# Unread products in TensorE's waits, and another order of the routing and of the last expert

## Chip, cores and metric

One core of one Trainium2 chip runs the program. The metric is the time of one execution on the device, in microseconds. Every time below is of the kernel before.

## What is computed

The reference is a stack of layers over 512 tokens of 1024 channels: a pooling layer and a latent-attention layer, each followed by a SwiGLU, a final norm, then differential attention and a routed mixture of experts. The change lies in the last part, which starts where differential attention has its heads:

```python
o = rmsnorm(o, subln) * (1 - lambda_init)          # 8 heads of 128
x = x + o.reshape(B, T, 1024) @ w_out              # da_out
xt = rmsnorm(x, norm_ffn)
logit_g, logit_e = xt @ w_group + b_group, xt @ w_router + b_router   # 4 groups, 16 experts
# the best group, the two best of its four experts, with shares
for e in range(16):
    y += combine[:, e] * ((silu(xt @ w_gate[e]) * (xt @ w_up[e])) @ w_down[e])   # 1024 -> 512 -> 1024
out = x + y
```

Everything is f32. Each weight product is made of three TensorE products: an operand is split into a high part (f32r) and the rest, and `product` adds low x high, high x low and high x high (lines 255 to 257), each 128 rows of weights against 512 columns.

## The kernel before

The 512 tokens are four tiles (T = 4) of 128. Every engine has its own list of instructions, written out by hand, and they meet by semaphores. PS is PSUM, eight banks of 512 columns. X holds the tokens.

**Attention's end and da_out.** VectorE scales the heads of a tile in two parts (`normal_part`, line 1776: six heads and two), in the order (0,0), (1,0), (2,0), (0,1), (1,1), (3,0), (2,1), (3,1) for (tile, part). TensorE turns each part into PS as it comes (line 1828). ScalarE copies a whole turned tile to AH (line 1837, high parts), VectorE makes AL (line 1846, low parts), and `route` starts the products of the output projection when tile 0 is there. They go tile by tile over four units of weights (`unit_into`, `unit_half`).

**Routing.** As tiles get ready, VectorE adds the residual (lines 2139, 2148), TensorE turns X (`turn_x`, line 1998) and makes 20 logits per token (`logits`, line 2007). The last tile is done in two halves. VectorE selects (`select`) and finds each token's place in its experts' lists (`place`) for a pair of tiles at a time. TensorE counts the places (lines 2047 to 2071) and turns them into a table of token numbers (`table`, line 2016) and a table of shares (line 2077). `row(t)` (line 2159) makes the normalized rows of tile t, which SyncE stores to moe_rows (line 1968) for the experts to gather; x_out (line 1964) stores X. `counts` holds the number of turns through the experts, one for these inputs; each engine loads it into a register (line 2327) and loops over it.

**Experts.** Six units of 1 MB of weights per expert (two each for gate, up and down), 96 in all. Eight are fetched in advance, and SyncE fetches another when VectorE has split the one in its slot (line 2339). ScalarE makes the high parts, `hi(k)` (line 2424), VectorE the low ones, `lo(k)` (line 2486), TensorE multiplies (`half_up` and `down`, 12 products a unit). GpSimd gathers 128 rows per expert (lines 2555, 2559), TensorE turns them (`turn_rows`, line 2357), ScalarE and VectorE copy high and low parts (`rows_out`, lines 2428 and 2491). ScalarE applies Silu (2435), VectorE multiplies gate by up (`gate_up`, 2498), TensorE turns h (`turn_h`, 2380), both copy it (`h_out`, 2439 and 2502), and after down ScalarE scales by the shares (`y_out`, 2445) and GpSimd adds the rows to the output (2570). Unit numbers: gate 88 and 89, down of expert 14 90 and 91, up 92 and 93, down 94 and 95 for the last expert.

The first steps of the experts' loop before are these, ScalarE above and VectorE below:

```python
hi(0); hi(1); hi(2); rows_out(0); hi(3); silu(0); rows_out(1); hi(4)
lo(0); lo(1); rows_out(0); lo(2); lo(3); rows_out(1)
```

VectorE comes to its lo(0) only after it has waited for the table of shares, copied it and loaded its count (lines 2293 to 2295, 2327).

Of the kernel before, what the change touches and what calls it, by code (L numbers as in the profile page):

```python
# [36 lines left out]
P = 128  # L37
# [8 lines left out]
SLOTS = 2  # L46
# [131 lines left out]
def build_program(nc, stream, experts, x, positions, gains, rows, lams, router, consts, band, out, moe_rows):  # L178
    ctx = ExitStack()
    with ctx:  # L180
# [78 lines left out]

        def square_tile(act, b, n, t, junk=None):  # L260
# [1555 lines left out]
        def da_out(block, O, normal):  # L1816
# [7 lines left out]
            def _(pe):  # L1824
                for n, (t, part) in enumerate(((0, 0), (1, 0), (2, 0), (0, 1), (1, 1), (3, 0), (2, 1), (3, 1))):
# [4 lines left out]
                    if part:  # L1830
                        mm.then_inc(heads_turned, 1)

# [26 lines left out]
        def expert_memory():  # L1859
# [43 lines left out]
            m.slot_share = sb("slot_share", [P, ROUNDS + 1, E])  # L1903
# [8 lines left out]

            m.prefetch = prefetch
            return m


        def route(block, m, qk_used, weighed, made, heads_lo):
# [27 lines left out]
            weight_ready = sem("expert_weight_ready")  # L1945
            u0 = U_DA_OUT
            last = T - 1
            ALF = AL[:, :, :].bitcast(F32)

# [32 lines left out]
            def _(pe):  # L1982
# [73 lines left out]
                turn_x(last, 0)  # L2056
                turn_x(last, 1)
# [4 lines left out]

# [8 lines left out]
                mm.then_inc(ranked, 1)  # L2071
                table(1).then_inc(tabled, 1)

# [8 lines left out]
            def _(act):  # L2082
# [36 lines left out]
                act.activation(m.group_exp[:, :, :], m.group_less[:, :, :], ACT.Exp).then_inc(exped, 1)  # L2119
                act.wait_ge(exp_ready, 2)  # L2120
# [3 lines left out]
            def _(dve):  # L2124
# [109 lines left out]
                invert(2)  # L2234
                row(2)
# [10 lines left out]
                dve.tensor_tensor(rstd[:, last:T], m.halves[:, 0:1], m.halves[:, 1:2], ALU.add).then_inc(sum_added, 1)  # L2246
                logit(2)
# [28 lines left out]
                dve.memset(m.slot_share[:, ROUNDS, :], 0.0)  # L2276
# [16 lines left out]
                dve.wait_ge(shares_tabled, 1)  # L2293
                then(dve.tensor_copy(m.slot_share[:, 0:ROUNDS, :].rearrange("p r e -> p (r e)"), PS[:, 7, 0:ROUNDS * E]))
                dve.tensor_copy(m.share_now[:, :], m.slot_share[:, 0, :]).then_inc(weight_ready, 1)

            return counted, index_ready, weight_ready, rows_stored, x_stored


        def run_experts(block, m, counted, index_ready, weight_ready, rows_stored, x_stored):  # L2300
# [22 lines left out]
            found, y = X[:, 0:2, :], X[:, 2:4, :]  # L2323

            def rounds_of(engine):
                engine.wait_ge(counted, 1)
                return engine.value_load(counts[0:1, 0:1], min_val=1, max_val=ROUNDS)
# [16 lines left out]
            def _(pe):  # L2344
                rounds = rounds_of(pe)
                with nc.Fori(0, rounds, engines=(mybir.EngineType.PE,), hint_back_edge=True) as r:
# [49 lines left out]
                    turn_rows(0)  # L2396
                    gate(0, 0)
                    gate(0, 1)
                    turn_rows(1)
                    for n in range(E):  # L2400
                        for part in range(2):
                            half_up(n, PS[:, 1, :], up_unit(n), part)
                        if n + 1 < E:
                            gate(n + 1, 0)
                        turn_h(n)
                        if n + 1 < E:
                            gate(n + 1, 1)
# [250 lines left out]
```

## Time and profile before

| | us |
|---|---|
| median of 3 runs | 1569.75 |
| lowest and highest | 1566.68, 1569.96 |
| the profiled execution's own time | 1566.38 |
| its span, first to last instruction | 1564.6 |
| attention, da_out and all before it | to 1181.5 |
| output projection and routing | 1181.5 to 1249.9 |
| experts' first product to last | 1260.7 to 1553.6 |
| last rows added, end | 1553.6 to 1564.6 |

Mean granted TensorE clock: 0.981 of full speed. The profile's times are from the span's start. The clock has two levels, 1.0 for 2.4 GHz and 0.5 for 1.2 GHz; a value between means that it changed in the stretch. A busy TensorE at the low level does half as much.

### The profile page before, as it was taken

To read this page: it belongs to the slowest core of one execution; us is meant where nothing else is said; L and a number is where in the kernel's file an instruction comes from. 1 tells how busy PE (TensorE), PEld (TensorE's weight loads), DVE (VectorE), ACT (ScalarE), POOL (GpSimd) and SP (SyncE) were. 2 spreads that over 40 slices of the span, in tenths; PEclk is the share of its full clock that TensorE was granted. 3 is DMA by queue.
4 is the path that set the end of the run, shared out by engine and by line. 5 is a ranking of instruction groups with operands and counts; after the bars stand their busy time and mean duration, and the time that the engine had idled before them with its cause. 6 is when DMAs were issued, how large, how long until landed. Compare 5 with 4: busy or idle time off the path is not lost.

```text
span 1564.6 us, 19025 instructions
## 1 busy us (share of the span) xinstructions
PE 1504.3 (96%) x7399; PEld 1244.3 (80%) x7399; DVE 780.5 (50%) x947; ACT 673.8 (43%) x854; POOL 79.5 (5%) x57
## 2 busy tenths in 40 slices
PE   8899999999899999999999999999899789999996
PEld 8888888888787788888888887788567778888874
DVE  6433333231566435333323216335684679899884
ACT  5322222212355424222322115433782368787773
POOL 0000000000000000000000000000130012111211
PEclk9999999999999999999999999999999789999998
DMA  6123232232230032323232232232132379999993
GB/s 243 61 101 107 80 107 85 104 104 98 81 108 28 1 121 67 115 88 107 80 107 105 84 121 81 98 108 81 33 120 120 149 273 384 384 390 393 387 380 96
DMA packets 36207, 226.18 MB, mean 145 GB/s; under 512 B 5271, under 2 KB 5527, under 8 KB 11824
## 3 DMA queue, kind: packets, MB, share of 16 engines
q1 hardware_dynamic: 31392, 212.06, 35.9%
q0 software_dynamic: 4608, 13.22, 3.6%
q8 instruction: 45, 0.74, 0.2%
q14 instruction: 18, 0.15, 0.0%
q10 hardware_dynamic: 144, 0.03, 0.0%
HBM read 215.22 MB, written 13.63 MB: 146 GB/s over the span
## 4 chain that ended last, share of the span: by engine, by line
PE 53%; DVE 5%; DMA 3%; issue 2%; ACT 2%; DVEq 0%; ACTq 0%; SPq 0%; POOLq 0%
PE PS L255 16%; PE PS L257 16%; PE PS L256 16%; DMA eraw<-experts 3%; PE PS L1648 1%; PE PS L2357 1%; DVE da_flat L1732 1%; PE PS L1659 1%; DVE WL L250 1%; PE PS L2007 1%; ACT WEH L2424 1%; PE PS L1668 1%; PE PS L1453 0%; DVE da_flat L1746 0%; DVE WEL L2486 0%
## 5 line engine op out<-in xcount | busy, mean ns | idle before, releaser
L250 DVE TENSOR_TENSOR WL<-raw,WH 128x2048 fp32r<-128x2048 f32 x93 | 213.9, 2300 | 432.1 <-ACT WH L245 432.1
L255 PE MATMUL PS<-AH,WL 128*128 128x512 f32 (+1 forms) x768 | 286.7, 373 | 4.3 <-DVE AL L303 4.3
L256 PE MATMUL PS<-AL,WH 128*128 128x512 f32 (+1 forms) x768 | 286.0, 372 | 0.0
L257 PE MATMUL PS<-AH,WH 128*128 128x512 f32 (+1 forms) x768 | 286.0, 372 | 0.0
L245 ACT ACTIVATE WH<-raw 128x2048 fp32r<-128x2048 f32 x93 | 177.6, 1910 | 240.9 <-PE PS L257 240.9
L2486 DVE TENSOR_TENSOR WEL<-eraw,WEH 128x2048 fp32r<-128x2048 f32 x96 | 217.2, 2286 | 20.1 <-ACT WEH L2424 19.9
L2424 ACT ACTIVATE WEH<-eraw 128x2048 fp32r<-128x2048 f32 x96 | 182.2, 1914 | 31.6 <-DMA eraw<-experts 16.7
L255 PEld LDWEIGHTS PS<-AH,WL 128*128 128x128 f32 x768 | 145.6, 190 | 29.5 <-DVE AL L303 4.5
L257 PEld LDWEIGHTS PS<-AH,WH 128*128 128x128 f32 x768 | 145.5, 189 | 25.2
L256 PEld LDWEIGHTS PS<-AL,WH 128*128 128x128 f32 x768 | 145.6, 190 | 24.9
L255 PE MATMUL PS<-WH,AL 128*128 128x512 f32 (+2 forms) x416 | 156.3, 376 | 8.0 <-DVE WL L250 7.6
L257 PE MATMUL PS<-WH,AH 128*128 128x512 f32 (+2 forms) x416 | 154.1, 371 | 0.0
L256 PE MATMUL PS<-WL,AH 128*128 128x512 f32 (+2 forms) x416 | 153.8, 370 | 0.0
L255 PE MATMUL PS<-WEH,AH 128*128 128x512 f32 x256 | 102.7, 401 | 5.5 <-DVE AH L2491 5.5
L257 PE MATMUL PS<-WEH,AH 128*128 128x512 f32 x256 | 100.9, 394 | 0.0
L256 PE MATMUL PS<-WEL,AH 128*128 128x512 f32 x256 | 100.6, 393 | 0.0
L255 PEld LDWEIGHTS PS<-WH,AL 128*128 128x128 f32 x416 | 79.3, 191 | 22.2 <-DVE WL L250 6.8
L257 PEld LDWEIGHTS PS<-WH,AH 128*128 128x128 f32 x416 | 79.3, 191 | 13.0
L256 PEld LDWEIGHTS PS<-WL,AH 128*128 128x128 f32 x416 | 79.4, 191 | 12.1
L255 PE MATMUL PS<-WH,f0FL 128*128 128x512 f32 x176 | 69.8, 396 | 0.0
L257 PE MATMUL PS<-WH,f0FH 128*128 128x512 f32 x176 | 69.6, 395 | 0.0
L256 PE MATMUL PS<-WL,f0FH 128*128 128x512 f32 x176 | 69.6, 395 | 0.0
(316 smaller groups left out, 2110.2 us busy)
## 6 DMA issues: line engine op xcount, KB each, us to landing
eraw<-experts SPq DMA_DIRECT2D x96, 1024.0 KB, 14.6
raw<-stream SPq DMA_DIRECT2D x94, 1024.0 KB, 4.8
out<-X SPq DMA_DIRECT2D x5, 512.0 KB, 2.7
moe_rows<-moe_rows_g SPq DMA_DIRECT2D x5, 512.0 KB, 2.7
X<-x SPq DMA_DIRECT2D x4, 512.0 KB, 5.3
ffn_row<-rows SPq DMA_DIRECT2D x2, 512.0 KB, 9.3
final_row<-rows SPq DMA_DIRECT2D x2, 512.0 KB, 6.0
cst<-consts SPq DMA_DIRECT2D x1, 739.5 KB, 13.5
```

What stands on the lines that cost most here:

```text
L245: act.activation(WH[:, u % SLOTS, :], raw[:, u % SLOTS, :], ACT.Copy).then_inc(unit_hi, 1)
L250: dve.tensor_tensor(WL[:, u % SLOTS, :], raw[:, u % SLOTS, :], WH[:, u % SLOTS, :].bitcast(F32), ALU.subtract).then_inc(unit_lo, 1)
L255: pe.matmul(acc, lhs_lo, rhs_hi, start=start, stop=False)
L256: pe.matmul(acc, lhs_hi, rhs_lo, start=False, stop=False)
L257: return pe.matmul(acc, lhs_hi, rhs_hi, start=False, stop=stop)
L1648: pe.matmul(PS[:, 2 * (i % 2) + m, 0:(q + 1) * P], QT[rows64, h, q * P:(q + 1) * P], KT[rows64, h, 0:(q + 1) * P], start=True, stop=True). ...
L1659: mm = pe.transpose(PS[:, 4 + j % 2, k * P:(k + 1) * P], buffer(j, 0)[:, k * P:(k + 1) * P], ident)
L1668: mm = pe.matmul(PS[:, 6 + h % 2, q * P:(q + 1) * P], turned_probs[:, j % 2, k * P:(k + 1) * P], V[:, k, h * P:(h + 1) * P], start=(k == 0 ...
L1732: dve.tensor_tensor_reduce(buffer(i, m), PS[:, 2 * (i % 2) + m, 0:w], const("alibi")[:, S - w:S], 2.0 ** (-8.0 * (h + 1) / H), -NEG * 1e8, ...
L2007: mm = pe.matmul(PS[:, 2 * t, 0:20], m.XT[:, t, c, :], m.wr[:, c, :], start=(c == 0), stop=(c == C - 1))
L2424: act.activation(WEH[:, k % ESLOTS, :], eraw[:, k % ERAW, :], ACT.Copy).then_inc(unit_hi, 1)
L2486: dve.tensor_tensor(WEL[:, k % ESLOTS, :], eraw[:, k % ERAW, :], WEH[:, k % ESLOTS, :].bitcast(F32), ALU.subtract).then_inc(unit_lo, 1)
```

## The change

It adds `keep_busy`: n products of 128 by 512 whose result nothing reads, written to a bank of PS that is not in use. Eight places call it, with 7, 2, 2, 5, 9, 6, 4 and 6 products, 41 in all. The other edits: `invert(2)` and `row(2)` move on VectorE from ahead of `place(0)` to behind the sums of the last tile; the table of shares is no longer copied to SBUF whole, but read from PS at the start of each turn through the experts; ScalarE loads its count earlier; `rows_out(0)` goes ahead of `hi(2)` and of `lo(1)`; in the last expert `hi(95)` goes ahead of `y_out(14)`, and `lo(95)` behind `gate_up` and `h_out`. The diff, cut to its core:

```diff
+        def keep_busy(pe, bank, n, some=None):
+            some = AL[:, 3, :] if some is None else some
+            for _ in range(n):
+                pe.matmul(PS[:, bank, :], some[:, 0:P], some[:, 0:512], start=True, stop=True)
...
@@ da_out, TensorE, after the turn of each (tile, part)
+                    if n == 2:
+                        pe.wait_ge(unit_lo, u0 + 1)
+                        keep_busy(pe, 6, 7, WH[:, u0 % SLOTS, :])
...
@@ expert_memory
-            m.slot_share = sb("slot_share", [P, ROUNDS + 1, E])
...
@@ route, TensorE
                 turn_x(last, 0)
+                keep_busy(pe, 0, 2, WH[:, (u0 + 3) % SLOTS, :])
                 turn_x(last, 1)
                 for t in (2, last):
                     logits(t, 0)
                     logits(t, 1)
                 table(0)
-
+                keep_busy(pe, 0, 2)
                 pe.wait_ge(selected, 3)
...
                 mm.then_inc(ranked, 1)
+                keep_busy(pe, 0, 5)
                 table(1).then_inc(tabled, 1)
-
+                keep_busy(pe, 0, 9)
                 pe.wait_ge(weighted_out, 1)
...
@@ route, ScalarE
                 act.activation(m.group_exp[:, :, :], m.group_less[:, :, :], ACT.Exp).then_inc(exped, 1)
+                act_rounds.append(m.rounds_of(act, counted))
                 act.wait_ge(exp_ready, 2)
...
@@ route, VectorE
                 select(0)
-                invert(2)
-                row(2)
                 place(0)
                 add_half(0)
...
                 dve.tensor_tensor(rstd[:, last:T], m.halves[:, 0:1], m.halves[:, 1:2], ALU.add).then_inc(sum_added, 1)
+                invert(2)
+                row(2)
                 logit(2)
...
-                dve.memset(m.slot_share[:, ROUNDS, :], 0.0)
...
                 ins.then_inc(weighted_out, 1)
-                dve.wait_ge(shares_tabled, 1)
-                then(dve.tensor_copy(m.slot_share[:, 0:ROUNDS, :].rearrange("p r e -> p (r e)"), PS[:, 7, 0:ROUNDS * E]))
-                dve.tensor_copy(m.share_now[:, :], m.slot_share[:, 0, :]).then_inc(weight_ready, 1)
...
@@ run_experts, TensorE
                     turn_rows(0)
+                    keep_busy(pe, 0, 6)
                     gate(0, 0)
...
+                        if n == E - 1:
+                            keep_busy(pe, 3, 4)
                         turn_h(n)
+                        if n == E - 1:
+                            keep_busy(pe, 3, 6)
...
@@ run_experts, ScalarE
-                rounds = rounds_of(act)
-                with nc.scalar.Fori(0, rounds) as r:
+                with nc.scalar.Fori(0, act_rounds) as r:
...
                     hi(1)
+                    rows_out(0)
                     hi(2)
-                    rows_out(0)
                     hi(3)
...
                     for n in range(E):
+                        after = up_unit(n) + 2
+                        if n == E - 1:
+                            hi(after + 1)
                         if n:
                             y_out(n - 1)
...
                         else:
-                            hi(after + 1)
                             h_out(n)
...
@@ run_experts, VectorE
                     lo(0)
+                    rows_out(0)
                     lo(1)
-                    rows_out(0)
+                    dve.wait_ge(shares_tabled, 1)
+                    dve.wait_ge(y_made, E * r + 1)
+                    dve.tensor_copy(share[:, :], shares[:, bass.ds(r, 1), :].rearrange("p r e -> p (r e)")
+                                    ).then_inc(weight_ready, 1)
                     lo(2)
...
                             lo(after)
-                            lo(after + 1)
                             gate_up(n)
                             h_out(n)
+                            lo(after + 1)
...
-                    dve.wait_ge(y_made, E * r + E + 1)
-                    dve.tensor_copy(share[:, :], m.slot_share[:, bass.ds(r + 1, 1), :].rearrange("p r e -> p (r e)")
-                                    ).then_inc(weight_ready, 1)
```

## Rows read from the trace of the kernel before

**Rows 1.** The page's part 1: busy us, share of the span and instructions of each engine.

```profile
PE 1504.3 (96%) x7399; PEld 1244.3 (80%) x7399; DVE 780.5 (50%) x947; ACT 673.8 (43%) x854; POOL 79.5 (5%) x57
```

**Rows 2.** The chain that ended last, in order: start us, us, what, xcount if merged.

```profile
1223.53 1.71 PE PS L2007 x16
...
1265.35 0.43 PE PS L256
...
1266.48 0.23 PE PS L256
```

**Rows 3.** Busy time by stretch: us, each engine's busy (x), PEclk, DMA share, GB/s.

```profile
1174.10:1177.40 3.30, 1.50 (x12) 1.03 (x11) 3.02 (x14) 0.42 (x2) 0.00 (x0) 1.00 0.93 360
1177.50:1180.80 3.30, 3.30 (x17) 3.10 (x16) 2.96 (x6) 1.84 (x2) 0.00 (x0) 0.50 1.02 415
...
1235.50:1241.10 5.60, 4.61 (x22) 4.48 (x22) 1.88 (x9) 2.63 (x3) 0.00 (x0) 0.50 0.47 187
...
1260.70:1266.10 5.40, 5.38 (x13) 4.22 (x14) 4.28 (x2) 0.00 (x0) 0.00 (x0) 0.50 0.98 357
...
1276.00:1530.00 254.00, 253.08 (x1198) 209.24 (x1197) 226.36 (x130) 202.27 (x144) 50.79 (x26) 1.00 1.02 385
...
1546.10:1549.40 3.30, 2.88 (x7) 2.33 (x8) 0.32 (x1) 0.00 (x0) 0.00 (x0) 0.50 0.00 0
```

**Rows 4.** Timeline of da_out: start us, us, engine line op out<-in xcount [idle before].

```profile
1177.17 4.10 PE L1828 MATMUL PS<-cst,da_flat 128*128 128x128 f32 x20 [1.54 <-DVE da_flat L1776]
...
1177.47 2.30 DVE L1776 TENSOR_TENSOR da_flat<-da_flat,da_head_stat 128x256 f32<-128x256 f32 x5
1178.96 4.25 ACT L1837 ACTIVATE AH<-PS,gain 128x1024 fp32r<-128x1024 f32 x4 [2.38 <-PE PS L1828]
...
1180.11 4.86 DVE L1846 SCALAR_TENSOR_TENSOR AL<-PS,gain,AH 128x1024 fp32r<-128x1024 f32 x4 [0.34 <-ACT AH L1837]
```

**Rows 5.** Timeline of the routing's end, columns as in rows 4.

```profile
1227.64 1.28 DVE L2159 SCALAR_TENSOR_TENSOR moe_rows_g<-X,rstd,final_row 128x1024 f32<-128x1024 f32 x1
...
1227.96 0.26 PE L2049 MATMUL PS<-route_both,route_ones 128*128 128x16 f32 x1
...
1228.95 8.81 SPq L1968 DMA_DIRECT2D moe_rows<-moe_rows_g  x2
...
1233.36 0.66 PE L1998 MATMUL PS<-cst,X 128*128 128x128 f32 x4 [0.74 <-DVE X L2148]
...
1233.86 5.38 PE L2007 MATMUL PS<-router_weights,moe_turned 128*128 128x20 f32 x32
...
1244.96 1.06 PE L2016 MATMUL PS<-route_told,AL 128*128 128x64 f32 x4 [2.57 <-DVE AL L2214]
...
1247.83 1.13 POOL L2555 DMA_INDIRECT X<-moe_rows,expert_index  x1 [73.94 <-issue]
...
1249.88 3.68 PE L2077 MATMUL PS<-moe_rows_g,AL 128*128 128x64 f32 x16 [3.86 <-DVE moe_rows_g L2289]
```

**Rows 6.** Timeline of the experts' start, columns as in rows 4.

```profile
1250.33 5.51 ACT L2424 ACTIVATE WEH<-eraw 128x2048 fp32r<-128x2048 f32 x3 [1.05 <-issue]
...
1253.35 1.91 PE L2357 MATMUL PS<-cst,X 128*128 128x128 f32 x8
...
1254.95 4.49 DVE L2486 TENSOR_TENSOR WEL<-eraw,WEH 128x2048 fp32r<-128x2048 f32 x2 [0.93 <-ACT WEH L2424]
1255.74 1.00 ACT L2428 ACTIVATE AH<-PS 128x1024 fp32r<-128x1024 f32 x1
...
1259.37 1.21 DVE L2491 TENSOR_TENSOR AH<-PS,AH 128x1024 fp32r<-128x1024 f32 x1
```

**Rows 7.** Timeline of VectorE alone in the last expert.

```profile
1541.46 2.29 DVE L2486 TENSOR_TENSOR WEL<-eraw,WEH 128x2048 fp32r<-128x2048 f32 x1 [0.51 <-ACT WEH L2424]
1543.67 0.68 DVE L2498 TENSOR_TENSOR expert_h<-expert_h,PS 128x512 f32<-128x512 f32 x1
```

**Rows 8.** Timeline of TensorE alone: the first down product of the last expert.

```profile
1546.52 0.77 PE L255 MATMUL PS<-WEH,AL 128*128 128x512 f32 x1 [1.46 <-issue]
```

More of the change, by code:

```diff
@@ L1911, in prefetch, with rounds_of @@
                     sp.dma_start(m.eraw[:, j, :], experts[0, j, :, :]).then_inc(m.landed[j], 16)
+            def rounds_of(engine, counted):
+                engine.wait_ge(counted, 1)
+                return engine.value_load(m.counts[0:1, 0:1], min_val=1, max_val=ROUNDS)
             m.prefetch = prefetch
+            m.rounds_of = rounds_of
             return m
@@ L1944, in route @@
             index_ready = sem("expert_index_ready")
-            weight_ready = sem("expert_weight_ready")
             u0 = U_DA_OUT
@@ L1948, in route @@
             ALF = AL[:, :, :].bitcast(F32)
+            act_rounds = []
             def cols(t):
@@ L2292, in _, with run_experts @@
                 ins.then_inc(weighted_out, 1)
-                dve.wait_ge(shares_tabled, 1)
-                then(dve.tensor_copy(m.slot_share[:, 0:ROUNDS, :].rearrange("p r e -> p (r e)"), PS[:, 7, 0:ROUNDS * E]))
-                dve.tensor_copy(m.share_now[:, :], m.slot_share[:, 0, :]).then_inc(weight_ready, 1)
-            return counted, index_ready, weight_ready, rows_stored, x_stored
-        def run_experts(block, m, counted, index_ready, weight_ready, rows_stored, x_stored):
+            return counted, index_ready, shares_tabled, rows_stored, x_stored, act_rounds[0]
+        def run_experts(block, m, counted, index_ready, shares_tabled, rows_stored, x_stored, act_rounds):
+            weight_ready = sem("expert_weight_ready")
             landed = m.landed
@@ L2323, in run_experts @@
             found, y = X[:, 0:2, :], X[:, 2:4, :]
+            shares = PS[:, 7, 0:ROUNDS * E].rearrange("p (r e) -> p r e", e=E)
             def rounds_of(engine):
-                engine.wait_ge(counted, 1)
-                return engine.value_load(counts[0:1, 0:1], min_val=1, max_val=ROUNDS)
+                return m.rounds_of(engine, counted)
             @block.sync
@@ L2457, in _ @@
                     for n in range(E):
+                        after = up_unit(n) + 2
+                        if n == E - 1:
+                            hi(after + 1)
                         if n:
                             y_out(n - 1)
-                        after = up_unit(n) + 2
                         if n + 1 < E:
```

## The prediction

> **What bounds the kernel now.** The first view is the page's table of engines. TensorE is busy 96% of the span, three others half of it or less [rows 1], so a change gains only where TensorE idles or runs slowly. The second view is the busy time by stretch, read for the granted clock [rows 3]. The clock is low in three places that the change touches: from 1177.5 in da_out, from 1235.5 until the experts' first products (1266.1), and in the last down products from 1546.1. Between them, from 1276 to 1530, TensorE is busy 253 of 254 us at the full clock, with the DMA engines at 1.02 of their share: that stretch can be moved, hardly shortened. The third view is the chain that ended last, for the price of one product: 0.43 us at the low clock, 0.23 at the full one [rows 2]; 16 logit products take 1.71 us (0.107 each) at the full clock. The last view is the timeline around each edit [rows 4 to 8]: it shows which wait ends last there.
>
> **da_out, seven products behind (2,0).** The turns start at 1177.17 and run through, 20 in 4.1 us, so at about 0.21 each; six of them are (2,0), over at about 1178.4. The next part, (0,1), is the first of VectorE's five pieces from 1177.47 and so is there by 1178 [rows 4]. There is no wait here to fill. The stall is ahead of (2,0) (1.54 us idle), where no product is put. With the clock low until about 1180.9 the seven take 2.5 us for 5.9 products and 0.25 for the rest, together 2.7. The two turns of (0,1) behind them are faster than before (0.22 instead of 0.43), so ScalarE's first copy, now at 1178.96, starts about 2.4 us later, then VectorE's (4.86 / 4 = 1.2 us a tile) and the first unit product. Bounds: 7 x 0.23 = 1.6 at the full clock, 7 x 0.43 = 3.0 at the low one. The 50 us of products behind it have no slack, so it is passed on: **+2.4**.
>
> In this stretch the clock came back with nothing but turns on TensorE: 3.3 of 3.3 us busy at 0.5 from 1177.5, and full from 1180.9 [rows 3]. The Trainium skill, TensorE: Matmul & The Clock Gate, section "Part 4: PE-mode transpose", says the opposite: that turns do not bring the full clock as products do. The trace disagrees. By that sentence the shares and turns at the experts' start could not bring the clock back either, and the whole sum would be -5.8 (first rival) where the row leads to -9.3.
>
> **Routing, order.** `row(2)` held VectorE until 1228.92 ahead of `place(0)`; the ranks were there at 1228.2 [rows 5], so `place(0)` and all behind it come about 0.6 earlier. `invert(2)` and `row(2)` (1.28 us and a column) now stand behind the last tile's sums, in the stretch in which VectorE waits for that tile's logits (TensorE makes logits from 1233.86 to 1239.24), so they cost nothing; without that cover they would cost some 1.4. On SyncE's queue `row_out(2)`, `row_out(3)` and `x_out(3)` follow them: stores that SyncE issued at 1228.95 and 8.8 us later; now both go out together at the later time, with x_out right behind. GpSimd's gather, which waits for them, starts at 1247.83 [rows 5], so more than 5 us are left for one more store. The second turn of the last tile (1233.36) starts at about 1232.8; two unread products (0.46) ahead of it fill the time until `add_half(1)`. The 32 logit products (5.38 us, the first 1.6 of them at the full clock) then have 0.6 us more of the full clock, so they end 0.6 + 0.6 earlier: **-1.2** (bounds: -0.6 without more clock; -2.4 if it is full throughout, 32 x 0.107 = 3.4). Two products ahead of the ranks (0.86) lie in VectorE's 1.7 us of `select`. Five fill 2.57 us of idle time (2.15 at the low clock), and nine fill 3.86 (3.87) [rows 5]: even at the low clock they cost nothing.
>
> **Experts' start.** Before, ScalarE began at 1250.33 (1.05 idle before it, of which loading the count about 0.75), VectorE's `lo(0)` at 1254.95, `rows_out(0)` ran on ScalarE at 1255.74 and on VectorE at 1259.37, and the first product followed at 1260.72 [rows 6]. Now VectorE does not wait for the shares. Step by step: ScalarE starts at 1250.33 - 0.75 - 1.2 = 1248.4; two `hi` (5.51 / 3 = 1.84 each) end at 1252.0. TensorE makes the shares from 1249.88 - 1.2 = 1248.7, 16 products in 3.7 us at the low clock [rows 5] or 1.9 at the full, then eight turns (1.91 or 1.0): over at 1251.6 at the full clock, 1254.1 at the low. ScalarE's rows (1.0) and VectorE's (1.2) end at 1254.3 or 1256.5. The six products (1.4 or 2.6) lie beside these. The first gate product comes 6.4 us earlier, or 4.2 (all counted from before, the -1.2 included). `lo(1)` ends 2.3 later, before the 12 products of the first unit (2.7) do. The wait for the shares' table stands behind it, with `lo(2)` queued there; the table is over by then, and y_made starts at one: nothing. `hi(2)` is a microsecond later and not needed for 5 us.
>
> The 24 gate products took 7.9 us, since 13 of them overlapped 5.4 us of low clock [rows 3]; at the full clock they take 24 x 0.227 = 5.5: -2.4. What pays for the clock: the nine, the shares, the turns and the six follow each other without a gap, at the low clock for some 11 us. In da_out 3.3 us of turns brought it back, so I take it as back for the shares. Not restored: -1.1, since the six start the busy stretch 2.6 us earlier. Sum here, with the routing: **-8.8** (low clock: -5.3). From then on the same list runs earlier; the first fetch is freed by `lo(0)`, some 4.7 us earlier, and fetches 9 to 12 are over before the next is due.
>
> **Last expert.** `gate_up` stood behind `lo(95)` until 1543.67 [rows 7], though the up products ended at about 1542.1: -1.5. The four products (0.9) fill the wait for `gate_up`, the six (1.4) the 1.5 us of copying h. The seven down products at 0.43 from 1546.52 [rows 8] cost 7 x 0.2 = 1.4 more than at the full clock: -1.4. `lo(95)` is done 2.3 us after `h_out`, before the 12 products of unit 94 (2.7 us). `y_out(14)` starts 1.9 later, and its scatter is long over when the last one is due. A copy of 16 columns of shares behind the loop goes too and is not counted. Sum **-2.9** (bounds: -1.4, if only one of the two comes, and -2.9).
>
> **Total.** 2.4 - 8.8 - 2.9 = -9.3. Against the profiled execution's own 1566.4 that is 1557.1. It was faster than all three runs shown, whose median stands 3.4 above it; taking the same offset, 1569.75 - 9.3 = **1560.4**. A measurement of this kernel can tell some 0.2% (3.1 us) from no change.
>
> **Rivals.**
> - *The clock is not back before the gate products* (0.27). For it: the stretch of 14 us from 1235.5 did not recover by itself, and the logit and share products are small. Against it: da_out's turns did recover. The sum is 2.4 - 5.3 - 2.9 = -5.8: 1563.9. The section of the Trainium skill named above points this way.
> - *The transfers pace the experts* (0.12). For it: their share is 1.02 for 254 us [rows 3]. Against it: TensorE never lacks work there. If so only the 4.7 us by which the first fetch moves arrive, and nothing at the end: 2.4 - 4.7 = -2.3: 1567.4, no change that counts.
> - *The unread products stand in the way* (0.06), the slower one. TensorE works in order, so a product that starts late in a wait delays what the wait was for. The place is the three long runs, 7 + 9 + 6 = 22, uncovered at 0.43: +9.4. What the new order gives without any clock is 4.2 at the start and 1.5 at the end. 9.4 - 5.7 = +3.7: 1573.5. It decides from (5.7 + 3.1) / 0.43 = 20 uncovered products on; rows 5 cover 14 in the routing even at the low clock, so this needs their waits to have shrunk.
> - *It does nothing*: the order cannot fail to free VectorE, so I give this no more than the rest (0.05, with what I have not seen).
>
> **Chances and range.** The forecast has 0.50. Faster by over 0.2%: forecast, first rival and a little of the rest, 0.80. Within 0.2%: 0.12. Slower: 0.08. The low end is the sum against the profiled execution with the logits at the full clock (1557.1 - 1.2, rounded down to 1555); the high end takes in the second rival, 1567.5.
>
> **What would show it.** Right: ScalarE's first da_out copy 1.5 to 3 us later; the clock 1.0 for the gate products of expert 0 and at the first down products of the last; no gap over 2.5 us between the first turns and the first gate product; idle TensorE time ahead of the experts gone from 5.5 us to below 2; `gate_up` of the last expert directly behind the up products. Wrong: first gate product less than 4 us earlier relative to the first unit product of da_out, or a stretch from 1276 on in which TensorE now waits for weights, or da_out's copy not later at all (then the clock did not fall there).

## The result and the profile after

The changed kernel takes 1558.3 us (median of 6, 1554.8 to 1562.7) against 1567.9 (median of 6, 1566.6 to 1570.0) of the kernel before: ratio 0.994, 95% interval 0.992 to 0.996. The profiled execution took 1556.9 us, and its span is 9.5 us shorter than before. The page of the changed kernel, its span line and the engines' busy time:

```profile
span 1555.1 us, 19103 instructions
...
PE 1508.2 (97%) x7440; PEld 1246.5 (80%) x7440; DVE 780.6 (50%) x944; ACT 673.9 (43%) x854; POOL 78.0 (5%) x57
```

TensorE has 41 more instructions, 3.9 us more busy time and 9.5 us less span [rows 1]. Busy time by stretch, with the columns of [rows 3]:

```profile
1176.10:1179.40 3.30, 1.50 (x12) 1.03 (x11) 3.02 (x14) 0.49 (x2) 0.00 (x0) 1.00 0.90 320
1240.30:1250.50 10.20, 9.48 (x26) 6.55 (x25) 8.29 (x44) 3.47 (x7) 1.69 (x2) 0.50 0.32 124
1250.60:1260.00 9.40, 8.04 (x47) 6.71 (x47) 7.26 (x5) 7.99 (x5) 1.34 (x2) 1.00 0.76 245
1276.00:1530.00 254.00, 252.97 (x1195) 209.34 (x1194) 225.45 (x128) 199.87 (x142) 50.74 (x26) 1.00 1.01 380
1538.30:1544.00 5.70, 5.67 (x24) 4.43 (x24) 2.13 (x1) 0.00 (x0) 0.00 (x0) 1.00 0.58 92
```

The stall ahead of (2,0) is the first line: 1.50 us busy of 3.3, as before, but here the clock did not fall behind it. The clock was low from 1240.3 to 1250.5, 10.2 us where it had been 30.7, full again for the shares, the turns and the first gate products, and full in the last down products (last line), which were partly at the low level before. The stretch from 1276 to 1530 looks as it did. Around da_out, in the columns of [rows 4]:

```profile
1179.24 0.87 PE L1834 MATMUL PS<-cst,da_flat 128*128 128x128 f32 x6 [1.54 <-DVE da_flat L1782]
...
1179.53 2.30 DVE L1782 TENSOR_TENSOR da_flat<-da_flat,da_head_stat 128x256 f32<-128x256 f32 x5
...
1179.87 1.85 PE L264 MATMUL PS<-WH 128*128 128x512 f32 x7
...
1181.56 1.69 PE L1834 MATMUL PS<-cst,da_flat 128*128 128x128 f32 x14
1181.97 4.13 ACT L1846 ACTIVATE AH<-PS,gain 128x1024 fp32r<-128x1024 f32 x4 [3.32 <-PE PS L1834]
```

The seven products (L264) stand between (2,0) and the other turns, and ScalarE's first copy waits for them: 2.73 us from the first turn of (2,0), where it was 1.79 although the clock was low there. The logits, and the start of the experts, with the first gate product of expert 0 in a fence of its own:

```profile
1236.28 3.65 PE L2020 MATMUL PS<-router_weights,moe_turned 128*128 128x20 f32 x32
...
1250.23 3.72 ACT L2441 ACTIVATE WEH<-eraw 128x2048 fp32r<-128x2048 f32 x2 [0.29 <-ACT spare L2433]
...
1250.56 2.00 PE L2092 MATMUL PS<-moe_rows_g,AL 128*128 128x64 f32 x16
1252.18 2.29 DVE L2504 TENSOR_TENSOR WEL<-eraw,WEH 128x2048 fp32r<-128x2048 f32 x1 [1.68 <-ACT WEH L2441]
...
1252.85 1.09 PE L2370 MATMUL PS<-cst,X 128*128 128x128 f32 x8 [0.30 <-DMA X<-moe_rows,expert_index]
...
1253.70 1.64 PE L264 MATMUL PS<-AL 128*128 128x512 f32 x6
1253.98 1.02 ACT L2445 ACTIVATE AH<-PS 128x1024 fp32r<-128x1024 f32 x1
...
1255.04 1.22 DVE L2509 TENSOR_TENSOR AH<-PS,AH 128x1024 fp32r<-128x1024 f32 x1 [0.57 <-ACT AH L2445]
```

```profile
1256.40 0.49 PE L255 MATMUL PS<-WEH,AH 128*128 128x512 f32 x1 [1.06 <-DVE AH L2509]
```

The 32 logits take 3.65 us instead of 5.38 and the 16 share products 2.00 instead of 3.68 [rows 5]. VectorE's `lo(0)` starts as soon as `hi(0)` is there, `rows_out(0)` follows at 1253.98 on ScalarE and 1255.04 on VectorE, and the gate starts at 1256.40 [rows 6]. The last expert, TensorE and then VectorE:

```profile
1535.27 1.07 PE L264 MATMUL PS<-AL 128*128 128x512 f32 x4
1536.21 0.66 PE L2393 MATMUL PS<-cst,expert_h 128*128 128x128 f32 x4
1536.62 1.64 PE L264 MATMUL PS<-AL 128*128 128x512 f32 x6
1538.33 0.47 PE L255 MATMUL PS<-WEH,AL 128*128 128x512 f32 x1
```

```profile
1535.47 0.69 DVE L2516 TENSOR_TENSOR expert_h<-expert_h,PS 128x512 f32<-128x512 f32 x1 [1.19 <-PE PS L257]
1537.54 0.69 DVE L2520 TENSOR_TENSOR AL<-PS,AL 128x512 fp32r<-128x512 f32 x1 [1.38 <-ACT AL L2456]
1538.14 2.28 DVE L2504 TENSOR_TENSOR WEL<-eraw,WEH 128x2048 fp32r<-128x2048 f32 x1
```

`gate_up` (1535.47) now follows the up products directly and `lo` comes last; the first down product starts 2.9 us behind the end of the up products, where it was 4.4 [rows 7, 8].

To compare executions, each stage is measured from its own start. The profiled execution of the changed kernel reached (2,0) at 1179.24 instead of 1177.17, through code that the change does not touch: in it the clock also fell for 3.4 us at 1120.8, in attention. Distances in us, as starts in the timelines (the up products' end is the start of the last one plus 0.39):

| from, to | before | predicted | changed |
|---|---|---|---|
| first turn of (2,0), first unit product | 4.37 | +2.4 | 5.32 (+0.95) |
| first unit product, first share product | 68.34 | -1.2 | 66.00 (-2.34) |
| first share product, first gate product | 10.84 | -5.2 | 5.84 (-5.00) |
| first gate product, second turn of rows | 8.15 | -2.4 | 5.57 (-2.58) |
| second turn of rows, end of the last up products | 273.25 | 0 | 273.47 (+0.22) |
| end of the up products, first down product | 4.40 | -1.5 | 2.90 (-1.50) |
| first down product, last one | 6.70 | -1.4 | 5.32 (-1.38) |
| sum of the changes | | -9.3 | -11.6 |

The 2.1 us by which this execution was late ahead of the change take the -11.6 to the -9.5 of the spans. The +0.95 of the first row sets an execution with the full clock in da_out against one in which it had fallen; the cost of the seven products is larger, as the runs below show.

### The profile page after: what moved, and what is told of

It is laid out like the page before. It is cut to its first block, busy times and chain, and to the rows that moved or that the text cites. A ratio compares the mean times of both kernels' runs of the same rounds, so it can differ in the third digit from the quotient of the medians.

```text
span 1555.1 us, 19103 instructions
## 1 busy us (share of the span) xinstructions
PE 1508.2 (97%) x7440; PEld 1246.5 (80%) x7440; DVE 780.6 (50%) x944; ACT 673.9 (43%) x854; POOL 78.0 (5%) x57
## 4 chain that ended last, share of the span: by engine, by line
PE 54%; DVE 4%; DMA 3%; ACT 1%; issue 1%; DVEq 0%; ACTq 0%; POOLq 0%; SPq 0%
PE PS L255 16%; PE PS L257 16%; PE PS L256 16%; DMA eraw<-experts 3%; PE PS L1654 1%; PE PS L2370 1%; PE PS L1665 1%; DVE da_flat L1738 1%; DVE WL L250 1%; PE PS L1674 1%; PE PS L1459 0%; PE PS L2020 0%; ACT WEH L2441 0%; DVE da_flat L1752 0%; PE PS L2393 0%
## 6 DMA issues: line engine op xcount, KB each, us to landing
cst<-consts SPq DMA_DIRECT2D x1, 739.5 KB, 13.7
```

## The experiments

Each was compared with the kernel before, in executions on the same chip, and the ratio is from that comparison; it is not exactly the quotient of the medians. The changed kernel itself stands at 0.994 (0.992 to 0.996). Where a time is given as so much above or below the changed kernel's 1558.3, it compares medians of different batches, the experiments' on different chips: the ratios give differences that are up to 1.3 us other, and of all the runs only the interval of the products alone lies clear of the changed kernel's. So what rests on one or two us is read from the profiles. Where a run's profile is used, its distances are those of the table above, and it is one execution of each kernel.

### Order alone, products alone

```diff
@@ order alone: the changed kernel, each of the eight calls
-                keep_busy(pe, ...)
@@ products alone: the kernel before, the same eight calls at the same places
+                keep_busy(pe, ...)
```

Order alone: 

> The changed kernel without any of the 41 unread products; the new order alone. Theory (order and products each bring about half): the routing's logits end 0.6 us earlier relative to the first unit product, the first gate product of expert 0 comes 4.2 us earlier relative to the shares' start of before, the clock is low from the logits to some of the gate products and again for the first down products of the last expert; without the seven products there is no 0.9 us in da_out. Sum about -6 us against before (ratio 0.996). Rival (the products do all of it): within 2 us of before. Rival (the products are in the way): faster than the changed kernel, below 0.994.

Measured: 1561.8 us, ratio 0.9965 (0.9952 to 0.9979). TensorE's timeline of that run around the experts' start:

```profile
1249.95 3.67 PE L2085 MATMUL PS<-moe_rows_g,AL 128*128 128x64 f32 x16 [3.85 <-DVE moe_rows_g L2297]
1253.41 1.91 PE L2363 MATMUL PS<-cst,X 128*128 128x128 f32 x8
1257.79 0.79 PE L255 MATMUL PS<-WEH,AH 128*128 128x512 f32 x1 [2.46 <-DVE AH L2497]
```

Shares in 3.67 us, turns in 1.91, first gate product 7.84 us behind the first share product instead of 10.84, and 4.18 us earlier behind the first unit product than before (expected 4.2). The last logit product started 1.2 us earlier behind the first unit product, where 0.6 was expected. The clock was low from 1236.8 to 1260.7, over the first gate products, as expected. Neither rival holds: the time is neither within 2 us of before nor below 0.994. Expected and not seen: the down products took 5.33 us, at the full clock, without any product of the change. So the last expert's clock was saved by the shorter wait, in this run at least.

Products alone: 

> The kernel before with all 41 unread products and the old order. Theory: the clock is back for the gate products of expert 0 (-2.4 us) and held in the last expert (-1.4), the shares and the turns at the full clock do not help, since VectorE still waits for its share copies and ScalarE runs three hi first; the seven in da_out cost 1 to 2.4. Sum -1 to -4 us against before (ratio 0.998). Rival (products in the way): slower than before by 2 us or more.

Measured: 1566.7 us, ratio 0.9987 (0.9976 to 0.9998). The last expert's down products took 5.30 us, as with the products they should. At the experts' start, by stretch:

```profile
1252.60:1259.00 6.40, 3.92 (x27) 3.19 (x26) 3.95 (x4) 6.40 (x5) 2.61 (x1) 1.00 0.35 124
1259.40:1266.00 6.60, 4.78 (x11) 3.79 (x12) 6.08 (x4) 0.93 (x1) 0.00 (x0) 0.50 0.97 377
```

The products had brought the clock back, but in the old order TensorE then waits for `lo(1)` and the rows: 3.92 us busy of 6.4, and the clock falls again for the gate products. From the first gate to the second turn of rows it takes 7.87 us (8.15 before, 5.57 with both). In da_out it stood 0.96 above the kernel before. The sum of -1 to -4 us that was expected came. Order alone saves 0.35% or 5.5 us, products alone 0.13% or 2.0, both 0.6% or 9.4. That is 1.9 more than the two together, less than the intervals can tell. The three profiles show no surplus in the whole: the distances of the table add up to -8.3 for the order alone, -3.9 for the products alone and -11.6 for both. By stages there is one. At the experts' start (first share product to second turn of rows) the order alone gives -4.2, the products alone -1.6 and both -7.6, since without the order the clock falls again at 1259.3. Against it, in the last down products either gives the whole -1.4 by itself, and in the routing (first unit to first share product) the order gives -1.2, the products -1.8 and both only -2.3.

### The seven products of da_out

```diff
@@ without them
-                    if n == 2:
-                        pe.wait_ge(unit_lo, u0 + 1)
-                        keep_busy(pe, 6, 7, WH[:, u0 % SLOTS, :])
@@ six, ahead of the turns of (2,0), in place of the seven
                 for n, (t, part) in enumerate(...):
+                    if n == 2:
+                        pe.wait_ge(unit_lo, u0 + 1)
+                        keep_busy(pe, 6, 6, WH[:, u0 % SLOTS, :])
                     pe.wait_ge(normal, n + 1)
```

Without: 

> The changed kernel without the seven products in da_out. Theory (they fill no wait): 1 to 2 us faster than the changed kernel; in the trace ScalarE's first copy of da_out starts 1.1 us (full clock) or 1.8 us (low clock) after the first turn of (2,0), where the changed kernel has 2.7. Rival (they hold the clock for the unit products behind them): the clock falls in da_out or at the first unit products, and the time is the same as the changed kernel's or up to 1.5 us longer.

Measured: 1556.6 us, ratio 0.9929 (0.9916 to 0.9942). ScalarE's first copy came 2.00 us behind the first turn of (2,0), with the clock low from 1179.3 (1.8 was expected at the low clock), so 0.73 earlier than in the changed kernel's execution with the full clock. The time, 1.7 us below the changed kernel, is as the theory says, though the intervals overlap. The clock did fall in da_out, as the rival said, but it fell with the first turn of (2,0), ahead of the place of the seven, and it does so in runs that have them too.

Six ahead: 

> The changed kernel with six unread products ahead of the turns of (2,0), in the 1.54 us in which TensorE waits there, instead of seven behind them. Theory: they are covered by the stall, the clock is held through the stall, and ScalarE's first copy starts about 1.1 us after the first turn of (2,0) against 2.7 in the changed kernel: 1.5 us faster than the changed kernel. Rival (it does not matter where they are): the same time as the changed kernel.

Measured: 1555.4 us, ratio 0.992 (0.9907 to 0.9933). The timeline of da_out in that run:

```profile
1179.46 1.63 PE L264 MATMUL PS<-WH 128*128 128x512 f32 x6
...
1181.25 1.55 PE L1837 MATMUL PS<-cst,da_flat 128*128 128x128 f32 x10 [0.16 <-DVE da_flat L1782]
...
1182.50 4.13 ACT L1846 ACTIVATE AH<-PS,gain 128x1024 fp32r<-128x1024 f32 x4 [1.84 <-PE PS L1837]
```

The six lie in the stall and end before the turns start, the clock holds, and ScalarE's copy starts 1.25 us behind the first turn, against 2.73. The first unit product follows at 3.93 (5.32 changed, 4.37 before). The low clock with the seven was caught in a run whose edit lies elsewhere (no products in the routing, below):

```profile
1178.82 1.54 PE L1834 MATMUL PS<-cst,da_flat 128*128 128x128 f32 x6 [1.54 <-DVE da_flat L1782]
...
1180.01 2.91 PE L264 MATMUL PS<-WH 128*128 128x512 f32 x7
...
1183.17 4.13 ACT L1846 ACTIVATE AH<-PS,gain 128x1024 fp32r<-128x1024 f32 x4 [4.94 <-PE PS L1834]
```

The clock fell behind the first turns of (2,0), the seven took 2.9 us with their latency, and ScalarE's copy came 4.35 us behind the first turn, the first unit product 6.94: +2.57 against the kernel before, whose clock also fell there. In the profiled executions that have the seven behind (2,0), the distance was 5.3 us in five and 6.9 in three. Without any it was 3.94 in the one execution that kept the full clock (order alone), and 4.37 and 4.58 in the two in which it fell (the kernel before, and without the seven). So, like against like, the seven cost 1.4 us at the full clock and 2.4 to 2.6 at the low one, and they do not keep the clock up, since it falls ahead of them. In both executions with the six ahead it was 3.9, as at the full clock without any: there they cost nothing. That they hold the clock is not shown: it held in both executions, but of the twelve profiled executions with nothing in that stall it held in seven.

### The products of the routing, and turns in their place

```diff
@@ without the five calls of the routing and of the experts' start
-                keep_busy(pe, 0, 2, WH[:, (u0 + 3) % SLOTS, :])
-                keep_busy(pe, 0, 2)
-                keep_busy(pe, 0, 5)
-                keep_busy(pe, 0, 9)
-                    keep_busy(pe, 0, 6)
@@ turns of a constant for the last three
+                keep_turning(pe, 0, 10)
+                keep_turning(pe, 0, 18)
+                    keep_turning(pe, 0, 12)
+        def keep_turning(pe, bank, n):
+            for _ in range(n):
+                pe.transpose(PS[:, bank, 0:P], ident, ident)
```

Without: 

> The changed kernel without the 24 unread products of the routing and of the experts' start (2, 2, 5, 9, 6); the seven and the last ten stay. Theory: the clock, once low in the logits, stays low until some of the gate products, as in the run with the order alone: first gate product 75 us behind the first unit product against 71.8 in the changed kernel, second turn 81.9 against 77.4. About 4 us slower than the changed kernel. Rival (the turns and the shares alone bring the clock back): the same as the changed kernel within 1 us.

Measured: 1562.7 us, ratio 0.9963 (0.9951 to 0.9976), 4.4 us above the changed kernel. By stretch:

```profile
1250.60:1260.00 9.40, 5.38 (x24) 4.98 (x24) 5.02 (x10) 7.07 (x6) 2.92 (x3) 0.50 0.59 192
1260.80:1264.00 3.20, 3.20 (x9) 2.46 (x8) 3.20 (x3) 1.68 (x1) 0.00 (x0) 0.50 0.42 100
```

Shares and turns alone did not bring the clock back: TensorE was busy for 5.38 of 9.4 us, and the clock was low beyond 1260.8. First gate product at 74.5 us from the first unit product (71.8 changed), second turn at 81.9 (77.4), as expected. Of these 4.5 us, 0.7 lie ahead of the shares, where the clock fell within the logits in this execution. The mean granted clock, which is on record for every execution, agrees: 0.981 to 0.986 in the ten of this run and 0.981 to 0.985 in the six of the order alone, against 0.986 to 0.990 in the six of the changed kernel.

Turns: 

> The changed kernel with 10, 18 and 12 turns of a constant in place of the 5, 9 and 6 unread products, which take as long (0.21 us a turn at the low clock against 0.43 a product). Theory, from da_out before the change (turns alone, and the clock came back): the clock comes back before the gate products as in the changed kernel, 71.8 us from the first unit product to the first gate product. Rival, by the Trainium skill, TensorE: Matmul & The Clock Gate, Part 4: PE-mode transpose: turns do not bring the full clock; then as without the products, about 75 us.

Measured: 1558.7 us, ratio 0.9938 (0.9914 to 0.9961); first gate product at 71.94 us. By stretch:

```profile
1247.00:1250.50 3.50, 3.17 (x16) 2.77 (x15) 2.92 (x15) 0.00 (x0) 0.00 (x0) 0.50 0.00 0
1250.50:1254.00 3.50, 3.41 (x20) 3.15 (x19) 2.17 (x12) 2.83 (x4) 2.12 (x2) 0.67 0.30 69
1254.00:1257.00 3.00, 2.63 (x24) 2.50 (x24) 2.19 (x1) 2.90 (x3) 0.00 (x0) 1.00 0.74 261
```

In the second line the clock changes in the middle, with ten and eighteen turns, the small table products and the first shares on TensorE and not one product of 512 columns. It stays full behind it. The sentence of the Trainium skill that was weighed in the prediction (TensorE: Matmul & The Clock Gate, "Part 4: PE-mode transpose"), that turns do not bring the full clock as products do, does not hold for f32 turns in this kernel. The profile does not show whether the engine's transpose mode, of which the sentence speaks, was on for them.

### The ten products of the last expert

```diff
-                        if n == E - 1:
-                            keep_busy(pe, 3, 4)
                         turn_h(n)
-                        if n == E - 1:
-                            keep_busy(pe, 3, 6)
```

> The changed kernel without the four and six unread products of the last expert. Theory of the prediction (they hold the clock there): the down products take 6.7 us as before instead of 5.3, 1.4 us slower. Rival, from the run with the order alone (the shorter wait holds it by itself): 5.3 us, the same time. In either case 2.9 us lie between the up and the down products.

Measured: 1558.1 us, ratio 0.9935 (0.9912 to 0.9958), the changed kernel's time. 2.89 us between up and down, 5.30 for the down products, at the full clock. With the run of the order alone and the one below, the clock held in all three executions without the ten. In the old order, with 4.4 us of waiting, it fell without them (6.70) and held with them (5.30, products alone), in one execution each.

With six products ahead of (2,0) as well (the edit shown above) and none in the last expert:

> The changed kernel with six unread products ahead of the turns of (2,0) instead of seven behind them, and without the ten of the last expert. Theory: da_out 3.9 us from the first turn of (2,0) to the first unit product instead of 5.3 to 6.9, the last expert the same (2.9 and 5.3 us): 1.5 to 3 us faster than the changed kernel, the same as the run with the six alone. Rival (the last ten hold the clock in some executions): slower than the run with the six alone by up to 1.4 us.

Measured: 1557.4 us, ratio 0.9932 (0.9912 to 0.9952). da_out 3.94 us, the last expert 2.89 and 5.34, as the theory says, but the time is not the 1.5 to 3 us below the changed kernel that was expected: 0.9 by the medians, and 2.0 above the run with the six alone, with overlapping intervals. The profiled execution shows two parts of its own loss: the clock fell in the logits at 1237.7 instead of 1240 to 1242, and the last logit product started 0.9 us later behind the first unit product (56.00 against 55.10 and 55.13); and from the second turn of rows to the last up product it took 274.47 us, 1.0 more than in the changed kernel. The rival (slower than the six alone) has the time on its side, but in the profiled execution the last expert's clock held without the ten, and no other one has a profile. So the difference stays open; when the clock falls differs between executions of one kernel and may account for it.

### The order of the rows, the wait for the shares, row(2)

```diff
@@ rows back
-                    rows_out(0)
                     hi(2)
+                    rows_out(0)
...
                     lo(0)
-                    rows_out(0)
                     lo(1)
+                    rows_out(0)
@@ wait first
+                    dve.wait_ge(shares_tabled, 1)
+                    dve.wait_ge(y_made, E * r + 1)
+                    dve.tensor_copy(share[:, :], ...).then_inc(weight_ready, 1)
                     lo(0)
                     rows_out(0)
                     lo(1)
-                    dve.wait_ge(shares_tabled, 1)
-                    dve.wait_ge(y_made, E * r + 1)
-                    dve.tensor_copy(share[:, :], ...).then_inc(weight_ready, 1)
@@ row(2) back
                 select(0)
+                invert(2)
+                row(2)
                 place(0)
...
-                invert(2)
-                row(2)
                 logit(2)
```

Rows back: 

> The changed kernel with rows_out(0) back behind hi(2) on ScalarE and behind lo(1) on VectorE. Theory: VectorE's rows wait for lo(1), which ends 2.3 us after lo(0), and ScalarE's for a hi of 1.9 us: the first gate product comes 2 to 3 us later behind the first unit product (74 to 75 instead of 71.8), and the time is 2 to 3 us longer, or 1.4 more where the longer wait lets the clock fall. Rival (the fetches pace the experts, so their start does not matter): the same time as the changed kernel.

Measured: 1561.3 us, ratio 0.9954 (0.9939 to 0.9969), 3.0 above the changed kernel. First gate product at 73.52 us (+1.7), and the clock fell again at 1257.8, so that the second turn came at 80.48 (+3.1). So of these 3.1 us the later rows are 1.7, and 1.4 are the clock that the shorter wait of the changed order keeps: from the first gate product to the second turn it took 6.96 us instead of 5.57.

Wait first: 

> The changed kernel with VectorE's wait for the shares and the copy ahead of lo(0). Theory (what kept lo(0) waiting before was this wait): lo(0) starts at the end of the shares' products, about 68 us behind the first unit product instead of 67.6, a small delay now that the shares are made at the full clock, and rows_out(0) about 0.5 us later: first gate product 72.0 to 72.8 instead of 71.8, the time up to 1 us longer. Rival (this wait is what the start hinges on): 3 us longer or more.

Measured: 1561.0 us, ratio 0.9949 (0.993 to 0.9969), 2.7 above the changed kernel by the medians and 1.4 by the ratios, more than expected. The timeline of the experts' start:

```profile
1251.33 3.67 PE L2092 MATMUL PS<-moe_rows_g,AL 128*128 128x64 f32 x16
...
1254.80 1.92 PE L2370 MATMUL PS<-cst,X 128*128 128x128 f32 x8
1255.27 0.17 DVE L2526 COPY expert_share<-PS 128x16 f32 x1 [3.99 <-PE PS L2092]
1255.39 2.29 DVE L2504 TENSOR_TENSOR WEL<-eraw,WEH 128x2048 fp32r<-128x2048 f32 x1
...
1256.75 1.02 ACT L2445 ACTIVATE AH<-PS 128x1024 fp32r<-128x1024 f32 x1 [2.02 <-PE PS L2370]
...
1257.81 1.23 DVE L2509 TENSOR_TENSOR AH<-PS,AH 128x1024 fp32r<-128x1024 f32 x1
```

The shares were made at the low clock (3.67 us, then the turns in 1.92), which came back only at 1259.7. `lo(0)` waits for the share copy, and starts at 1255.39 instead of directly behind `hi(0)`. But it holds up nothing here: VectorE's rows (1257.81) follow ScalarE's (1256.75), which waited for the turns. So in this execution the 2.0 us by which the first gate product is late come from the low clock. Up to the shares TensorE's list is the changed kernel's and came at the same distances (first share product 65.98 us behind the first unit product, 66.00 in the changed kernel, where the clock was back by then). So the nine products do not restore it in every execution. The mean granted clock was 0.985 in three of the four executions of this run, the profiled one among them, and 0.986 to 0.990 in the changed kernel's six. The long low stretch may thus be usual here and belong to the edit, though the profile shows no way from the edit to it; that stays open.

row(2) back: 

> The changed kernel with invert(2) and row(2) back ahead of place(0). Theory: the logits start 0.6 us later behind the first unit product (52.3 instead of 51.7) and everything to the first gate product follows (72.4 instead of 71.8). Rival (they are covered in either place): 51.7 and 71.8.

Measured: 1558.7 us in a single time, so only the profile counts. The logits start 52.28 us behind the first unit product instead of 51.72: the 0.6 us expected. The first gate product came at 73.74, 1.9 later; the clock had fallen earlier (1237.8), so the further 1.3 us cannot be put down to the edit.

### Twice the products

The other counts are 4, 4, 10, 18, 12, 8 and 12 for 2, 2, 5, 9, 6, 4 and 6.

```diff
-                        keep_busy(pe, 6, 7, WH[:, u0 % SLOTS, :])
+                        keep_busy(pe, 6, 14, WH[:, u0 % SLOTS, :])
...
```

> The changed kernel with twice the number of unread products at each of the eight places (14, 4, 4, 10, 18, 12, 8, 12). Theory: the counts of the change just fill the waits, so those added lie on the path: 1.6 us in da_out, 0.5 ahead of the logits, 0.5 to 0.9 ahead of the ranks, 1.1 to 2 ahead of the table, 2 to 3 ahead of the shares, 0.5 to 1.4 ahead of the gate products, 2.3 in the last expert, 8 to 12 us in all, so no faster than the kernel before. Rival (unread products cost little anywhere): within 3 us of the changed kernel.

Measured: 1561.9 us, ratio 0.9958 (0.9944 to 0.9971), 3.6 us above the changed kernel. By the distances: da_out 6.90 (+1.6, at the full clock), first unit to first gate product 73.58 (+1.7), end of the up products to first down 4.84 (+1.9): 5.3 us in the profile. 8 to 12 were expected. The 41 added would take 9.4 us at the full clock and 17.6 at the low one, and at the clocks of this execution about 10.8, so about half is covered. The miss is in the routing and at the experts' start, where 4.6 to 7.8 us were expected and 1.7 came: the clock was low for 6.8 us instead of 10.2, back at 1250.2, and the eighteen products ahead of the shares ran at the full clock and took 4.2 us, as long as the nine of the changed kernel at the low one. The theory's "no faster than before" is wrong, and the rival's bound of 3 us is about met (3.6 by the medians, 2.8 by the ratios). The mean granted clock of this kernel is the highest of all (0.988 to 0.991) and its time is not the best: the clock by itself is not the aim.

## Why the prediction was right, point by point

**Total.** The forecast was 1560.4 us and -9.3; measured were 1558.3 and -9.6. The range (1555 to 1567.5) holds it. Most of the 2.1 us between the two times is the starting point, 1569.75 as the median of three and 1567.9 as that of six. That the changes agree within 0.3 us is in part luck: in the profiled execution two terms came out 1.5 and 1.1 us better than forecast, both by where the clock fell in it, and its sum is -11.6.

**da_out, +2.4: the mechanism right, the size by the clock.** The seven products fill no wait, and they delay ScalarE's first copy. The term assumed the clock low there, as in the trace of before. In executions where it fell, +2.57 was measured against the kernel before; in the changed kernel's own profile it did not fall, and it was +0.95, with ScalarE's copy 0.94 us later instead of the 1.5 to 3 that the prediction named as a sign. At equal clocks the price is 1.4 us (5.32 against 3.94, full; the prediction's bound was 1.6) or 2.4 to 2.6 (low). The better place was the one the prediction named, the stall ahead of (2,0): 3.93 us, and the fastest median of all (1555.4). The intervals of that run (0.9907 to 0.9933) and of the changed kernel (0.992 to 0.9959) overlap, so the 1.4 us are shown by the profile and only suggested by the times.

**Routing, -1.2: mis-sized, -2.34.** The 0.6 us of order was exact (0.60 at the logits' start). The other 0.6 was the bound case of -2.4: the clock stayed full through all 32 logits in the profiled execution (3.38 us between the first start and the last). The predicted value occurred as well: in the run with the order alone the last one started 1.2 us earlier than before.

**Experts' start, -5.2 and -2.4: right**, -5.00 and -2.58, and each part stood up alone: order alone gave 4.18 of 4.2 at the first gate product, and without the products most of the second part was gone (7.38 us from the first gate product to the second turn, 5.57 with them, 8.15 before). The clock came back before the shares, as assumed, in the profiled run. It does not in every execution (1259.7 in the run with the wait first). The earlier loading of ScalarE's count was not taken back by itself; in the profile the idle time ahead of `hi(0)` went from 1.05 to 0.29 us, the 0.75 of the prediction.

**Last expert, -2.9: the sum right, one cause wrong.** The 1.5 is the order, whose two edits there (`hi(95)` and `lo(95)`) were not separated. The 1.4 was put down to the ten products; without them it was there as well in three executions, and the time of the run without the ten was the changed kernel's. So the shorter wait does it. That the products hold the clock in the old order rests on one execution with them and one without.

**Rivals.** *The transfers pace the experts*: from the second turn of rows to the last up product it took 273.25 us before and 273.47 after a start that was 7.6 us nearer to the shares, so the whole gain was passed on. Over the runs this distance varied between 271.6 and 274.7, without an order in it that the edits explain. It goes with the number of places from 1266 to 1535 in which TensorE waited for VectorE (for h, or for the low part of a unit): none in the execution with 271.6, one with 272.3, two with 273.0 to 273.2, three with 273.3 to 274.0, four or five with 274.4 to 274.7. So the prediction's "TensorE never lacks work there" is not quite true; what makes VectorE late there was not followed up. *The products stand in the way*: true of the seven alone, at 1.4 to 2.6 us; 41 more of them cost 3.6 us, not the price of 22 uncovered in the change. *The clock is not back*: not in the changed kernel's profile, nor by the mean clock of its six executions (0.986 to 0.990, against 0.981 to 0.985 with the order alone); true of the execution with the wait first.

## What to carry to other kernels

Where TensorE's clock falls with its waits, shorten the wait first: the order of instructions on two other engines kept the clock in the last expert at no price, in all three executions without the ten unread products there. Put an unread product into the wait itself, ahead of the instruction that waits, and look at what stands behind it: the seven here stood behind the wait and cost 1.4 to 2.6 us, the six ahead of it nothing. And measure such a change by distances within the profile, comparing stages at the same clock, since the clock falls at other places from execution to execution and moves the total by more than one of these edits.

## What was not expected of the hardware

The clock of identical code differs between executions. In attention, ahead of every edit, it fell for 3.4 to 6.9 us at about 1120, at about 1135, at both, or not at all, and the first turn of (2,0) came between 1176.3 and 1181.8 us: at 1176.3 and 1177.2 in the two executions with 13.7 us of low clock ahead of it, at 1180.6 to 1181.8 in the three with 24. The times of one kernel spread by 7.9 us (1554.8 to 1562.7); 5.5 can come from there. And 28 f32 turns restored the full clock as well as 14 products of 512 columns.
